# Two TensorE loops written out, and three identity transposes added at two places

## The reference

```
first block, twice:   u = rmsnorm(h) @ w_in            (7 parts)
                      ya = silu(layernorm(conv31(a_val * sigmoid(a_glu)))) * silu(a_z)
                      yb = window_attention(q, k, v, bias, sink) * silu(b_z)     16 heads of 64
                      h  = h + [ya, yb] @ w_out
                      h  = h + rmsnorm(p @ w_pe) * sigmoid(h @ w_pg)
                      then rmsnorm(h)
second block:         fox: causal attention with a forget gate, 32 heads of 64, gate, @ fox_w_out
                      swa: causal window attention with rotary and sinks, 32 query heads, gate, @ swa_w_out
                      then rmsnorm
```

## Time and profile before

| what | value |
|---|---|
| median of three runs | 1758.4 us (1757.22 to 1760.55) |
| the profiled execution, own time | 1758.62 us |
| span of the profiled execution | 1756.8 us |
| TensorE busy | 1737.4 us, 99% |
| VectorE, ScalarE, GpSimd busy | 74%, 51%, 2% |
| mean granted TensorE clock | 0.999 |
| share of the chain that ended last: PE | 90% |

### The profile page before, as it was taken

The page is one execution under the profiler, slowest core; times in us unless marked ns, Lnnn a source line. Parts: engine busy times, 40 slices in busy tenths (PEclk is TensorE's granted clock), DMA queues, the critical chain, the costliest instruction groups (busy, mean ns, idle before and its releaser), DMA issues.

```text
span 1756.8 us, 35798 instructions
## 1 busy us (share of the span) xinstructions
PE 1737.4 (99%) x14389; PEld 1668.2 (95%) x14389; DVE 1307.2 (74%) x2087; ACT 904.0 (51%) x1326; POOL 38.9 (2%) x48
## 2 busy tenths in 40 slices
PE   8999999999999999999999999999999999999998
PEld 7999999999999999999999898998989999999986
DVE  7999899977779987998776764656555666677655
ACT  5433665555544465546465463545455553665553
POOL 0000000000000000000000110000100000000000
PEclk9999999999999999999999999999999999999999
DMA  7676655555666665556556666655655556555564
GB/s 235 192 216 186 192 149 175 194 192 194 197 185 216 197 200 145 156 185 205 187 193 188 205 196 189 194 183 165 215 166 181 192 180 180 164 168 166 171 196 136
DMA packets 200092, 326.21 MB, mean 186 GB/s; under 512 B 14912, under 2 KB 66320, under 8 KB 199822
## 3 DMA queue, kind: packets, MB, share of 16 engines
q1 hardware_dynamic: 197085, 320.85, 58.5%
q10 hardware_dynamic: 2864, 3.36, 0.6%
HBM read 320.42 MB, written 2.69 MB: 184 GB/s over the span
## 4 chain that ended last, share of the span: by engine, by line
PE 90%; DVE 6%; ACT 1%; issue 1%; SPq 1%; DMA 1%; POOL 0%; ACTq 0%; DVEq 0%; POOLq 0%
PE g L495 70%; PE g L504 11%; DVE w_lo L917 2%; PE att L614 2%; PE att L659 2%; PE att L638 2%; DVE cacc L1163 1%; ACT w_hi L1546 1%; DVE u L1042 1%; ACT u L1555 0%; PE att L566 0%; SPq L308 0%; PE att L495 0%; DMA stage<-in_w_in_dram 0%; PE g L525 0%
## 5 line engine op out<-in xcount | busy, mean ns | idle before, releaser
L917 DVE TENSOR_TENSOR w_lo<-stage,w_hi 128x1024 fp32r<-128x1024 f32 x577 | 704.1, 1228 | 368.5 <-ACT w_hi L1546 367.7
L1546 ACT CAST w_hi<-stage 128x1024 fp32r<-128x1024 f32 x577 | 602.2, 1054 | 619.0 <-PE g L495 418.0
L495 PE MATMUL g<-a_hi,w_hi 128*128 128x256 f32 x2496 | 699.2, 280 | 1.2 <-DVE a_lo L1097 1.0
L495 PE MATMUL g<-a_lo,w_hi 128*128 128x256 f32 x2496 | 691.1, 277 | 0.0
L495 PE MATMUL g<-a_hi,w_lo 128*128 128x256 f32 x2496 | 691.1, 277 | 0.0
L495 PEld LDWEIGHTS g<-a_hi,w_hi 128*128 128x128 f32 x2496 | 469.9, 188 | 8.8 <-issue 7.3
L495 PEld LDWEIGHTS g<-a_lo,w_hi 128*128 128x128 f32 x2496 | 469.1, 188 | 0.0
L495 PEld LDWEIGHTS g<-a_hi,w_lo 128*128 128x128 f32 x2496 | 468.9, 188 | 0.2
L495 PE MATMUL g<-b_hi,w_hi 128*128 128x256 f32 x1440 | 401.1, 279 | 0.0
L495 PE MATMUL g<-b_hi,w_lo 128*128 128x256 f32 x1440 | 398.4, 277 | 0.0
L495 PE MATMUL g<-b_lo,w_hi 128*128 128x256 f32 x1440 | 398.4, 277 | 0.0
(11 more groups left out here) (232 smaller groups left out, 1387.1 us busy)
## 6 DMA issues: line engine op xcount, KB each, us to landing
stage<-in_fox_w_in_dram SPq DMA_DIRECT2D x128, 512.0 KB, 4.2
stage<-in_w_in_dram SPq DMA_DIRECT2D x112, 512.0 KB, 3.8
stage<-in_swa_w_in_dram SPq DMA_DIRECT2D x72, 512.0 KB, 3.9
stage<-in_w_in_dram SPq DMA_DIRECT2D x128, 256.0 KB, 3.1
stage<-in_w_out_dram SPq DMA_DIRECT2D x64, 512.0 KB, 4.3
stage<-in_w_pg_dram SPq DMA_DIRECT2D x64, 512.0 KB, 4.1
stage<-in_fox_w_out_dram SPq DMA_DIRECT2D x32, 512.0 KB, 4.3
stage<-in_swa_w_out_dram SPq DMA_DIRECT2D x32, 512.0 KB, 4.4
```

Source lines behind the costliest of these rows:

```text
L495: mm = pe.matmul(acc[:, j * S:(j + 1) * S], w[:, slot, c0 + j * P:c0 + (j + 1) * P], xx[:, k, :], start=st and m == 0 and j % 2 == 0, stop ...
L917: dve.tensor_tensor(w_lo[:, slot, :], stage[:, slot, :], w_hi[:, slot, :].bitcast(F32), ALU.subtract).then_inc(*t.inc("w_split"))
L1546: act.copy(w_hi[:, slot, :], stage[:, slot, :]).then_inc(*t.inc("w_rounded"))
```

## The change

Two loops of TensorE become plain Python loops, so that their three turns stand in the instruction stream one after the other with constants for wait values; the loops of the other engines stay. In each lot of kind "full" the slot of the fourth turning ends with `settle(MB[:, 0:P], 2)`. After the product of `ln_sum(0)` comes `settle(TB[:, 0:P], 1)`; the increment of `ln_bc` stays on the product.

```
             def heads(kind, values, at=0, extra=()):
                 work = {at + 2 * i: [turn(kind, i)] for i in range(GH // 2)}
+                if kind == "full":
+                    work[at + GH - 2].append(lambda: settle(MB[:, 0:P], 2))
                 work[at + GH] = list(extra) + [attend(kind, i, values) for i in range(GH // 2)]
...
-                            mm = pe.matmul(MB[:, 0:S], ones[:, :], mean[:, :], start=True, stop=True)
+                            pe.matmul(MB[:, 0:S], ones[:, :], mean[:, :], start=True, stop=True).then_inc(*t.inc("ln_bc"))
+                            settle(TB[:, 0:P], 1)
                         else:
...
-                        mm.then_inc(*t.inc("ln_bc"))
+                            mm.then_inc(*t.inc("ln_bc"))
...
-            with t.loop(pe, "fox", 3):
+            for _ in range(3):
                 fox_attention()
                 chunk("T", A, 0)
                 chunk("T", A, 1)
...
-            with t.loop(pe, "swa", 3):
+            for _ in range(3):
                 chunk("T", A, 0, work=swa_scores())
                 chunk("T", A, 1, work=heads("causal", swa_values, 7))
```

## The result

| | median us | from, to | runs | ratio to before, 95% interval |
|---|---|---|---|---|
| before, beside the changed kernel | 1757.57 | 1753.33 to 1765.84 | 12 | 1 |
| after | 1761.47 | 1760.09 to 1766.52 | 12 | 1.0026 [1.0015, 1.0038] |

The change makes the kernel 4.6 us slower by the ratio, 3.9 us by the medians. The forecast was 1758.0 us and no measurable change. The median lies inside the range; the direction was missed.

What follows compares the result with a forecast made beforehand. TensorE, busy 99% of the span, was taken as the bound. Loops -3.81, stops +4.7, spacing -1.0 and mean's transpose -0.5 sum to -0.6 us on 1758.62, giving 1758.0 us; range 1753.5 to 1762.5.

Steps and rivals of the forecast that it cites:

- the loops' term: Fox loop's first way back on TensorE: writing the loops out removes a gap and slower running behind it, -3.81 us.
- The stop after the fourth turning: In four full lots TensorE waits for ScalarE's two copies, then runs two transposes: 1.18 us a lot, +4.7 us.
- The spacing behind the second lot: First layer's second lot: added transposes bring 228 matmuls from the long spacing to the short one, -1.0 us.
- The prediction's bound on the other side: Spacing term: the transposes bring the other three lots to the long spacing for a stretch of 84, +1.1 us.
- The transpose after the mean: Behind ln_sum(0): one transpose brings 84 matmuls to the short spacing, 0.25 us a layer, -0.5 us for two layers.
- The stop that does not show: Rival, behind the fourth turning: copies done sooner or wait met elsewhere, 0.8 for 4.7, 1754.1 us; chance 0.12.
- the gap that stays: Rival, fox loop: gap still at 1086, caused by another engine's loop or a transfer, 1761.8 us; chance 0.06.
- the jump rule taken whole: Rival, both loops: each of the four jumps costs a gap's 3.06 us, 1748.8 us; chance 0.02.
- rival 2: Fox turns: spacing is drawn anew and the long one takes hold, two turns of four give 1763.0 us; chance 0.10.

Runs made afterwards that it cites:

- the loops alone: Kernel before with both TensorE loops, fox and last attention, written out and nothing else: 1756.39 us, ratio 0.9995.
- fox alone: Kernel before with only the fox loop written out, the last attention's loop kept: 1757.36 us, ratio 0.9995.
- the second new profile of the kernel before: Kernel before, unchanged, second of three new profiled executions: 1763.98 us.
- the 12 waits: Kernel before with twelve already-met waits ahead of TensorE's first wait, only moving later code: 1765.86 us, ratio 1.0049.
- The first of the new profiles of the kernel before: Kernel before, unchanged, first of three new profiled executions: 1754.51 us.
- the kernel with the stops alone: Kernel before with only the two transposes behind each full lot's fourth turning added: 1769.50 us, ratio 1.0068.
- The changed kernel without the stops: Changed kernel whose two transposes wait only for the last reader of their bank, not ScalarE's copies: 1757.85 us, ratio 0.9995 to the kernel before.

## Why the prediction was wrong

**The step that failed is the loops' term, -3.81 us.** The prediction said: "The price is read from whole turns: turn 2 takes 1183.89 - 1083.59 = 100.30 us with the gap before it, turn 3 takes 1280.38 - 1183.89 = 96.49 us." The reading of that execution was right, and so was the cause, TensorE's own stream at the jump: no gap where the loop is written out, and nine more packets with each gap. What failed is to take it as paid in every execution. The gap is in one of four profiled executions of the kernel before, and taking the loops out is worth 0.9 us by two kernels (the loops alone and fox alone, both 0.9995), and both intervals take in no change at all. The second half of the error was hidden by a coincidence: the profiled execution, 1758.62 us, stood near the median of three runs, 1758.4, and the prediction took that as leave to carry a term of this execution over to all of them. An execution without the gap can reach the same time and more by the longer spacing, as the second new profile of the kernel before did.

That the gap depends on where the loop's code lies is shown by the 12 waits: the same work at the same time, two gaps, and all five runs at 1764.37 us or more. Why this code is at an edge in the kernel before is not shown. The Trainium skill ("Runtime: NRT & Kernel Launch", section "Instruction fetch mechanics") gives TensorE 128 KiB of instruction memory, filled in blocks of 16 KiB. A turn of six packets of 16.4 KB, some 98 KB, would fit by that figure, as an estimate. The traces agree so far: in the kernels with 94 packets both jumps back fetch nothing, since the two copies that are written out add twelve packets. By the two-page window of the same section every one of these jumps had to fetch; the traces do not agree with it for TensorE. What decides between keeping and fetching again, for one position and for one execution, and why it is nine packets for a turn of six, stays open.

The prediction also did not see that the edits are not independent: with the loops kept, each of the two other edits brings two gaps (12 and 8 us slower alone). It is likely that the loops written out are what keeps the changed kernel at 4 us; no run has both other edits with the loops kept.

**The stop after the fourth turning, +4.7 us: right.** From rows 4 x 1.23 = 4.9 us; by runs 5.4 us for the stops and 5.8 for stops and transposes. Of its parts, the latency was 0.15 us and not 0.05 (the copies end at 200.22 + 1.07 = 201.29, TensorE starts at 201.44); the copies began 0.64 us after the turning's start, as they did before the change (0.63).

**The spacing behind the second lot, -1.0 us: wrong, in its reason and in its size.** The stretch stays at 117.9 ns behind the two added transposes. Three settling transposes, those after `attend`, stand right in front of it, and they stood there before the change too:

```profile
262.16 0.48 PE att L566 x3
262.64 26.88 PE g L495 x228
```

So the prediction's own stretch spoke against its reason. So does the changed kernel's longest one in the second layer, at the long spacing right behind a single settling transpose (115.61 us for it in the kernel before):

```profile
841.98 0.11 PE att L566
842.09 120.14 PE g L495 x1020
```

In the changed kernel without the two transposes, which is the kernel before up to this place, the stretch begins at 113.7 ns; its row of the chain:

```profile
263.39 9.55 PE g L495 x84
```

In the kernel before itself it begins short in two of four profiles. What a stretch draws here differs between executions of one kernel; what sets it is not shown.

Nor would the short spacing have paid. Where the stretch begins short, its row ends after 84 matmuls because the chain goes over to VectorE, and TensorE then waits for w_lo. The first of the new profiles of the kernel before has it at both layers' second lots:

```profile
PE g L495 <- DVE w_lo L917: 0.8, 2, 0.4
```

By the starts of the matmuls, the first 276 behind the first layer's second lot take 32.54 to 32.56 us where they begin short and 32.66 or 32.67 us where they are long: 0.1 us, not 1.0.

The prediction's bound on the other side came instead: the 288 matmuls behind the `attend` of a layer's first lot, with the next scores among them, take 39.55 us in place of some 39.11, at the long spacing. That is so in all four places with the stops (two layers of the changed kernel and of the kernel with the stops alone), and in 3 of the 24 others: 0.9 us for two layers.

**The transpose after the mean, -0.5 us: the spacing was right, the gain is not there.** Here the short spacing does follow the added transpose: the 84 matmuls run at 113.3 ns in all eight places that have it (four kernels, two layers) and at 117.8 ns in all twenty that do not. But TensorE then comes to `ln_sum(1)` earlier than VectorE's mean is ready, a wait that the prediction left out. The changed kernel without the stops has it in both layers:

```profile
PE att L747 <- DVE mean L1243: 0.5, 2, 0.3
```

In the first layer of the changed kernel the wait is absent: from the end of the product to the stretch of 324 it is 336.41 - 320.32 = 16.09 us for 331.69 - 314.86 = 16.83 before, -0.74 us, the next 48 matmuls being short too. In the second layer the gain ends in the wait of 0.3 us at L749, shown above. From the product's start to the 324 it is 16.95 to 17.21 us in seven of the eight places, and 16.96 to 17.21 us in the twenty without the transpose. So the gain showed in one place of eight.

**The sum again.** With the loops at -0.9 for -3.81, 4.9 for the stops, the spacing at +0.9 for -1.0 and the mean between -0.7 and 0, it is +4.2 to +4.9 us over the kernel before; measured are 3.9 us by medians and 4.6 by the ratio with its interval from 2.6 to 6.7.

**The rivals.** The stop that does not show, the gap that stays and the jump rule taken whole all fall: the stops are there, the gap is gone, and looped jumps mostly cost nothing. Of the second, "drawn anew" is right for the spacing, but it is as true of the kernel before; the fox turns themselves stayed at 96.49 us. The slower side that came was none of the four: a gain that most executions had no need of, so that the stops' cost stood nearly alone. (From the prediction's figures rival 2 passes 0.2% at some 900 matmuls, (1761.9 - 1758.0) / 4.3 ns, not at 950.)

## What to carry to other kernels

A stall that one profiled execution shows once in several like places (one way back of four) may not be in the next execution at all. Before it is counted as a gain, profile the same kernel again, and weigh it by how often it comes. Where a kernel loops over a long body on TensorE, the count of instruction packets tells whether the body was fetched again, and any edit ahead of the loop, even one that costs no time, can change that; compare packets before a slower or faster run is put down to the edit itself. Before a shorter stretch of one engine is counted as a gain, see what ends it: here the chain went over to VectorE at two places, and TensorE lost there in waiting what it had won. A wait that stands in the slot of the instructions it waits for costs the whole latency: the same transposes with a narrower wait were 0.22 us instead of 1.23.

## What the runs showed of the hardware that was not expected

- Moving a program's code by 12 waits that were already met costs 8.6 us here; 128 or 256 of them cost only their own issue, 0.054 us each ((15.24 - 8.33) / 128).
- After a gap of 2.8 to 2.9 us TensorE was granted 0.50 of its clock for some 6 us with 12 waits ahead, but 1.00 right behind the gap of 3.06 us in the first profile of the kernel before. With the layer norm's transpose alone one execution has both: 0.58 and 0.56 for 4 us behind the first gap, 1.00 behind the second, each of 2.8 us. The window in the kernel before:

```profile
1086.00:1090.00 4.00, 3.35 (x15) 2.76 (x16) 1.18 (x1) 0.29 (x1) 0.00 (x0) 1.00 0.60 177
```

- 256-column matmuls run at 113.3 or 117.8 ns at the same granted clock of 1.00, held for more than 1000 in a row, and for these long stretches the choice differs between executions of one kernel; it is worth up to 5 us a stretch, more than the change. No run here tells what sets it.
